# Two output gates of block 2 in seven quarter products, and the sums of weight slices by accumulating transfers

## What is computed

```
p = h @ w_in
c_val, c_gate, c_og, ts, r_og, g_conv, g_rwkv = split(p)
# convolution branch
u = layernorm(conv31(c_val * sigmoid(c_gate)))
y_c = (silu(u) * silu(c_og)) @ w_conv_out
# recurrence branch: r, k, v and the decay from ts
o = groupnorm(rwkv7(r, decay, k, v, kk, kk * a)) + bonus
y_r = (o * silu(r_og)) @ w_rwkv_out
# g_conv and g_rwkv gate y_c and y_r, and w_out follows
```

## Time and profile before

| | |
|---|---|
| median of 3 runs | 1057.2 us |
| the profiled execution's own time | 1056.02 us |
| its span, first to last instruction | 1054.2 us |
| granted TensorE clock, mean | 0.998 |
| busy in the span: TensorE, VectorE, ScalarE, GpSimd | 99%, 72%, 23%, 12% |
| a stage of block 2, pairs 2 to 6 | 46.6 us |
| TensorE's share of the chain that ended last | 97% |

### The profile page before, as it was taken

One profiled execution on the slowest core, in us unless ns is written; L12 is line 12 of the kernel. 1 busy time (PEld: TensorE's weight loads), 2 busy tenths in 40 slices (PEclk: granted clock), 3 DMA queues, 4 the chain that ended last, 5 costly groups with the idle time before them and its releaser, 6 DMA issues.

```text
span 1054.2 us, 21653 instructions
## 1 busy us (share of the span) xinstructions
PE 1043.1 (99%) x8888; PEld 902.0 (86%) x8888; DVE 757.2 (72%) x1714; ACT 237.5 (23%) x630; POOL 126.8 (12%) x174
## 2 busy tenths in 40 slices
PE   9999999999999999999999999999999999999997
PEld 8899899998988499999644988898898989887983
DVE  4488776867743477777757788777878778777875
ACT  4032222213300120010101432323232232324101
POOL 1101000000045121100250010010100001010052
PEclk9999999999999999999999999999999999999999
DMA  8786566552377447564556333233333322161261
GB/s 263 267 307 237 207 198 220 193 186 88 121 228 231 159 71 251 196 191 161 176 194 229 90 111 101 88 114 101 101 94 108 121 81 82 41 242 41 81 160 40
DMA packets 72309, 162.68 MB, mean 154 GB/s; under 512 B 18930, under 2 KB 33170, under 8 KB 72211
## 3 DMA queue, kind: packets, MB, share of 16 engines
q1 hardware_dynamic: 71202, 159.67, 46.1%
q10 hardware_dynamic: 1008, 1.63, 0.5%
HBM read 160.17 MB, written 1.11 MB: 153 GB/s over the span
## 4 chain that ended last, share of the span: by engine, by line
PE 97%; DVE 2%; DMA 1%; issue 0%; ACT 0%; POOL 0%; DVEq 0%; ACTq 0%; POOLq 0%
PE bank L861 27%; PE bank L1016 18%; PE bank L492 13%; PE bank L927 6%; PE bank L1042 4%; PE bank L678 3%; PE bank L793 2%; PE bank L836 2%; PE bank L1188 2%; PE bank L1200 2%; PE bank L1357 2%; PE bank L1079 1%; PE bank L989 1%; PE bank L995 1%; PE bank L570 1%; PE bank L523 1%
## 5 line engine op out<-in xcount | busy, mean ns | idle before, releaser
L1016 PE MATMUL bank<-hT,slots 128*128 128x256 f32 x896 | 204.9, 382 | 0.0
L1016 PEld LDWEIGHTS bank<-hT,slots 128*128 128x128 f32 x896 | 167.6, 190 | 23.3 <-issue 0.3
L861 PE MATMUL bank<-hT,slots 128*128 128x128 f32 x832 | 103.4, 275 | 0.0
L2513 DVE SCALAR_TENSOR_TENSOR arena<-padA,par,arena 128x256 f32<-128x256 f32 x232 | 102.8, 504 | 0.0
L861 PEld LDWEIGHTS bank<-hT,slots 128*128 128x128 f32 x832 | 97.9, 192 | 0.7 <-issue 0.7
L861 PE MATMUL bank<-arena,slots 128*128 128x128 f32 x768 | 95.6, 275 | 0.0
L861 PEld LDWEIGHTS bank<-arena,slots 128*128 128x128 f32 x768 | 90.9, 192 | 0.5
L492 PE MATMUL bank<-hT,slots 128*128 128x256 f32 x336 | 74.4, 380 | 0.0
L492 PEld LDWEIGHTS bank<-hT,slots 128*128 128x128 f32 x336 | 63.4, 190 | 9.2 <-issue 0.8
L492 PE MATMUL bank<-arena,slots 128*128 128x256 f32 x304 | 66.2, 379 | 0.4 <-DMA slots<-in_w_br 0.4
L492 PEld LDWEIGHTS bank<-arena,slots 128*128 128x128 f32 x304 | 57.6, 190 | 8.6 <-DMA slots<-in_w_br 0.8
(11 more groups left out here) (480 smaller groups left out, 1891.1 us busy)
## 6 DMA issues: line engine op xcount, KB each, us to landing
slots<-in_w_rwkv SPq DMA_DIRECT2D x72, 512.0 KB, 3.6
slots<-in_w_heads SPq DMA_DIRECT2D x64, 512.0 KB, 4.5
slots<-in_w_gu SPq DMA_DIRECT2D x44, 512.0 KB, 4.5
arena<-in_ada_w SPq DMA_DIRECT2D x24, 512.0 KB, 5.2
slots<-in_w_down SPq DMA_DIRECT2D x20, 512.0 KB, 4.4
slots<-in_w_br SPq DMA_DIRECT2D x32, 256.0 KB, 2.8
slots<-in_w_out SPq DMA_DIRECT2D x16, 512.0 KB, 4.1
slots<-in_w_y SPq DMA_DIRECT2D x16, 512.0 KB, 6.9
```

The source lines that it names most:

```text
L861: end = e.matmul(out, w[:, k * P:(k + 1) * P], rhs[:, k, :], start=k == 0, stop=k == 3)
L1016: end = e.matmul(proj(w, q), slot[w][:, k * P:(k + 1) * P], hT[:, k, :], start=k == 0, stop=k == KT - 1)
L2513: e.scalar_tensor_tensor(out=o, in0=src, scalar=w, in1=o, op0=ALU.mult, op1=ALU.add).then_inc(*dve.step(f"tap{n}.{q}"))
```

## The change

For pairs 0 to 6 the output gates OGP and ROG are made like the branch gates, by seven products of quarters. `own_gate_pair` becomes `own_pair(e, what, q)`, called for "o" and then for "g". The raw gates are put together in a new tile `oraw`: one copy on ScalarE, one addition on VectorE in gap 5 (`first_output_sums`), three in gap 6 (`other_output_sums`); the two tanh and the two gating operations come behind these. Signs of `bt` change, so that all sums of weight slices are plain additions, and two results come out negated (the scale of -0.5 and the subtraction take care of it).

VectorE makes no slice sum any more. SyncE loads three more quarters of 256 KB for each gate pair (`load_sums`), and GpSimd's queue issues four accumulating transfers of 256 KB for each: eight in a stage, between `Z0` and `csum`. `FILL` goes from 70 units used to 68, and a few taps are dealt out anew.

```diff
-FILL = (0, 12, 11, 12, 11, 13, 13)
-FILL_FIRST = (14, 9, 9, 10, 10, 10, 10)
+FILL = (0, 11, 11, 11, 11, 12, 12)
+FILL_FIRST = (13, 9, 9, 9, 9, 9, 10)
...
+        oraw = carve(4, P)
+        osum = [carve(512) for _ in range(2)] + [adaA[:, 2 * D + 512:]]
...
+                elif w in (OGP, ROG) and q < LAST:
+                    e.wait_ge(*dve.upto(f"oq11.{q}" if w == OGP else f"oq1221.{q}"))
...
-        def own_gate_pair(e, q):
+        def own_pair(e, what, q):
+            even, odd = PAIR_OF[what]
+            one, two = gate_banks_of(q) if what == "g" else output_banks_of(q)
+            s2, s3, s4 = bs if what == "g" else osum
...
                 if n == 2:
                     e.wait_ge(*dve.upto("bt4"))
-                    e.wait_ge(*dve.upto(f"bs4.{q}"))
+                    e.wait_ge(*added[what][1].upto(f"sum2.{q}"))
                 if n == 3:
-                    read_out(e, PLACE[GRP, q] - 2)
+                    e.wait_ge(*added[what][0].upto(f"sum1.{q}"))
+                    read_out(e, PLACE[odd, q] - 2)
+                if n == 4:
+                    e.wait_ge(*added[what][2].upto(f"sum3.{q}"))
+                if n == 5:
+                    e.wait_ge(*added[what][3].upto(f"sum4.{q}"))
...
-                for w in (OGP, ROG):
-                    yield from projection(e, w, j)
-                yield from own_gate_pair(e, j)
+                yield from own_pair(e, "o", j)
+                yield from own_pair(e, "g", j)
...
             if more:
-                slice_sum(3)
-                og_silu()
+                first_output_sums()
                 operand_b(e, j + 1)
...
             if more:
-                rg_silu()
+                other_output_sums()
                 operand_r(e, j + 1)
...
             if more:
-                taps(e, j + 1, 13 if chain else 10, 18)
+                og_silu()
+                rg_silu()
+                taps(e, j + 1, 14 if chain else 10, 17)
...
+        def slice_additions(e, what, j):
...
+            e.wait_ge(*in_slot[odd].upto(f"rw{odd}.{j}"))
+            e.dma_start(s1, from_odd[:, 512:], accum_op=ALU.add).then_inc(*added[what][0].step(f"sum1.{j}"))
+            e.wait_ge(*in_sum[what][1].upto(f"a11.{j}"))
+            e.dma_start(s3, from_odd[:, 0:512], accum_op=ALU.add).then_inc(*added[what][2].step(f"sum3.{j}"))
+        def later_additions(e, what, j):
...
+            e.dma_start(s2, s1, accum_op=ALU.add).then_inc(*added[what][1].step(f"sum2.{j}"))
+        def last_additions(e, what, j):
...
+            e.dma_start(s4, s2, accum_op=ALU.add).then_inc(*added[what][3].step(f"sum4.{j}"))
...
+            if j < LAST:
+                for additions in (slice_additions, later_additions, last_additions):
+                    for what in "og":
+                        additions(e, what, j)
...
+            def load_sums(what, j):
...
+                e.dma_start(s2, src[:, 0:512]).then_inc(*in_sum[what][0].step(f"a11.{j}"))
+                e.dma_start(s3, src[:, 0:512]).then_inc(*in_sum[what][1].step(f"a11.{j}"))
+                e.dma_start(s4, src[:, 512:]).then_inc(*in_sum[what][2].step(f"a12.{j}"))
```

More of the change, by code:

```diff
@@ L166, in build @@
         in_ada = [tally(f"loads_into_ada{n}", 16) for n in range(2)]
+        in_sum = {w: [tally(f"loads_into_sum{n}_{w}", 16) for n in range(3)] for w in "og"}
+        added = {w: [tally(f"additions_into_sum{n}_{w}", 16) for n in range(4)] for w in "og"}
         to_g = tally("stores_to_g", 16)
@@ L427, in build @@
         LAST = R_PAIRS - 1
+        PAIR_OF = {"o": (OGP, ROG), "g": (GCP, GRP)}
         NEXT, OWN = (VAL, GATE, K_, R_, V_), (OGP, ROG, GCP, GRP)
@@ L1043, in own_gate_pair @@
                     if k == 3 and n in (2, 6):
-                        end.then_inc(*pe.step(f"b126.{q}" if n == 2 else f"p{GRP}.{q}"))
+                        end.then_inc(*pe.step(f"{what}126.{q}" if n == 2 else f"p{odd}.{q}"))
                     if k % 2:
@@ L1775, in act_rwkv @@
                     act_pad(e, "v", V_, j + 1)
-                half_gate(OGP, OG[:, j, :], "og.th", j)
+                e.wait_ge(*pe.upto(f"o126.{j}"))
+                e.activation(oraw[:, 1, :], output_banks_of(j)[0][:, 0, :], ACT.Copy).then_inc(*act.step(f"op1.{j}"))
             if levels:
                 inverted(4)
-            if more:
-                half_gate(ROG, rg[j % 3], "rg.th", j)
-            if levels:
                 e.wait_ge(*pe.upto(f"tok.{j}"))
                 e.activation(tokBK[j % 2], chunks(bank[4][:, :]), ACT.Copy).then_inc(*act.step(f"tok.{j}"))
+            if more:
+                for n, (to, name) in enumerate(((OG[:, j, :], "og.th"), (rg[j % 3], "rg.th"))):
+                    e.wait_ge(*dve.upto(f"oq1221.{j}"))
+                    e.activation(to, flat(oraw[:, 2 * n:2 * n + 2, :]), ACT.Tanh, scale=0.5).then_inc(*act.step(f"{name}.{j}"))
             if last:
@@ L2663, in dve_rwkv @@
             if more:
-                slice_sum(0)
                 dve_decays(e, j + 1)
             if levels:
-                taps(e, j, *((23, 28) if not j else (27, CONV2) if more else (22, 27)))
+                taps(e, j, *((23, 28) if not j else (26, CONV2) if more else (22, 27)))
             if j and more:
@@ L3270, in sp_rwkv @@
                       OGP: BY_PRODUCT, GCP: DOWN - 2}
+            DONE_BY = {GCP: GRP, OGP: ROG}
+            def load_sums(what, j):
+                if j == 0:
+                    e.wait_ge(*pe.upto("lora"))
+                even, (s2, s3, s4) = PAIR_OF[what][0], bs if what == "g" else osum
+                src = a["w_rwkv"][j * NR + even, :, :]
+                e.dma_start(s2, src[:, 0:512]).then_inc(*in_sum[what][0].step(f"a11.{j}"))
+                e.dma_start(s3, src[:, 0:512]).then_inc(*in_sum[what][1].step(f"a11.{j}"))
+                e.dma_start(s4, src[:, 512:]).then_inc(*in_sum[what][2].step(f"a12.{j}"))
             def load_projection(w, j):
-                e.wait_ge(*pe.upto(f"p{GRP if w == GCP else w}.{j - 1}" if j else free[w]))
+                e.wait_ge(*pe.upto(f"p{DONE_BY.get(w, w)}.{j - 1}" if j else free[w]))
                 if j == 0 and w in summed:
@@ L3282, in sp_rwkv @@
                 load_projection(w, 1)
+            for what in "og":
+                load_sums(what, 0)
             for j in range(1, R_PAIRS):
@@ L3288, in sp_rwkv @@
                     load_projection(w, j)
+                    if w in (ROG, GRP) and j < LAST:
+                        load_sums("o" if w == ROG else "g", j)
         def sp_out(e):
```

89 lines of the change are left out of this document (54 added, 35 removed).

## The result

The changed kernel takes **1058.57 us** (median of 20 runs, 1057.86 to 1060.47); beside it the kernel before takes 1056.82 us (20 runs, 1055.56 to 1059.56). The ratio is 1.0018, 95% interval 1.0012 to 1.0025: 1.75 us slower where 4.5 us faster was forecast, above the upper end of the range. The profiled execution took 1058.07 us, its span is 1056.3 us.

The account below looks back on a forecast made before the run. TensorE, busy 99% of the span, was taken as the bound: 1056.0 - 4.6 + 0.1 for small waits = 1051.5 us for a profiled execution, with the median 1.2 us above it 1052.7 us, range 1051.2 to 1056.4 us.

Parts of the forecast that it names:

- The size of the gain: TensorE's rows per pair: 6.91 us of removed products become 6.26 us, 0.65 us less per pair, 4.6 us for seven.
- Nothing waits behind GpSimd's queue but `csum`: GpSimd's queue: behind the transfers only csum, read only in the last pair, and the next `Nd.m`, 40 us on.
- VectorE gains about 1.5 us against 0.43: Gaps 2 and 3: three slice sums of about 0.65 us go, one 0.41 us tap comes; gap 3 loses a unit.
- Gap 1, 0.11 us late: Gap 1 loses 0.43 us against 0.32 idle, so `state(1)` comes 0.11 us late; priced at nothing, 0.8 us at worst.
- Gap 4, nothing: Gap 4 keeps its units and gets a tap ahead of a ScalarE wait: nothing, at worst 0.4 us x 7.
- Gaps 5 and 6: VectorE's play at the ends of gaps 5 and 6: 0.29 and 0.57 us stay, so both cost nothing.
- `oq1221`: Added TensorE wait in gap 6: 0.36 us spare less a handover, taken as nothing; pair 0's wait 0.5 us.
- Transfers: Accumulating transfers taken at 4 us, between 2.8 and 9.5; the fifth in time for gap 5; DMA share about 0.6.
- Issues beside VectorE: GpSimd's eight issues beside VectorE in gaps 1 to 3: between nothing and 2.6 us a stage, taken as nothing.
- Rival 2: Gain returns as VectorE waits (gaps 1, 3, 5, `oq1221`), 0.2 to 0.6 us a pair: 1054.1 to 1057 us; chance 0.13.
- Rival 1: GpSimd's issues hold up VectorE's taps, 1.5 us a pair reaching TensorE: 1063 us; chance 0.12.
- Rivals 3 and 4: Third: transferred sums arrive late, 1081 us, chance 0.03. Fourth: rows don't get cheaper by the count, about 1057, chance 0.02.

Follow-up runs that it names:

- experiment 1: Changed kernel with csum moved ahead of the last four accumulating transfers of a stage in GpSimd's program: 1052.63 us, ratio 0.9963 to the kernel before.
- experiment 4: Changed kernel without its 56 accumulating transfers, TensorE waiting for the plain loads instead: 1053.02 us, ratio 0.9966 to the kernel before.
- experiment 3: Kernel before with csum alone held until VectorE has made kp, beside the six taps of gap 3: 1056.61 us, ratio 1.0.
- experiment 6: Kernel before with csum held until kp and one 256 KB accumulating transfer issued right ahead of it: 1059.77 us, ratio 1.0031.
- experiment 5: Changed kernel with csum behind all transfers and held until the fourth of gap 3's seven taps: 1056.85 us, ratio 1.0003 to the kernel before.
- experiment 7: Kernel before with csum held until ScalarE's square of k is done, no issue ahead: 1056.9 us, ratio 1.0004.

## Why the prediction was wrong

**The size of the gain was right.** 32 rows for 56, 0.65 us a pair: with both losses removed a middle stage is 45.96 us (45.95 was forecast). Pairs 1 to 6 together take 275.27 us there (649.21 to 924.48); the forecast is 279.19 - 6 x 0.65 = 275.29.

**Where the changed kernel's 282.20 us come from** is then a subtraction: csum early takes it to 276.57 (647.92 to 924.49), so csum's place costs 5.6 us; the longer gap 1 takes it to 275.27, so the missing play costs 1.3. Together 6.9 us against a gain of 3.9 in these six pairs. The split depends on the order: the longer gap 1 alone takes it to 279.86, which is worth 2.3, and csum's place is then worth 4.6.

**The step that failed first: "Nothing waits behind GpSimd's queue but `csum`".** It asked who needs csum's result (no one, until the last pair), and not what csum does to its neighbour when it runs 8.0 us later in the stage (at 755.08 us, 13.5 into its stage, before; at 763.69, 21.6 into it, now). Part of the price was on the table: the earlier trace rows had shown operations of GpSimd slowing taps, and I applied it to the issues alone, which by experiments 1 and 4 cost nothing by themselves. That csum costs 1.0 to 1.3 us right behind an issue, and not 0.48, no row of before could tell.

**The step that failed second: "VectorE gains about 1.5 us against 0.43"** in gaps 2 and 3. Taking work away gains time only up to the next wait. In the kernel before ScalarE's `own.k` ended at 761.07 and `shift` began at 761.10: the slice sums just filled a wait that was there anyway. Without them VectorE is idle for 1.83 us, and `shift` starts at the same 19.53 us. The whole relief was worth nothing, while TensorE's need came two units, 0.86 us, earlier and gap 3 got one more tap, 2.85 - 2.46 = 0.39 us. Play of 1.05 us became a lack of 1.05 - 0.86 - 0.39 = -0.2, and with csum early a stage is 46.15 us instead of 45.95. It is this that made csum's collision count in full; with the old play csum cost a stage nothing alone (experiment 3), and 0.24 us behind an issue (experiment 6).

**Point by point, the rest.**
- Gap 1, 0.11 us late, priced at nothing: no wait there. Gap 4, nothing: right.
- Gaps 5 and 6: 0.30 and 0.53 us of idle time against 0.29 and 0.57.
- `oq1221`: no wait in pairs 1 to 6; pair 0's stall 0.5 us, as worked out.
- Transfers: I took 4 us between 2.8 and 9.5; they took 4.3 to 8.1. In time for TensorE, as said. But the size mattered in a way that I had not asked: it sets when csum runs. In pair 6, with quicker ones, csum falls into VectorE's idle time and costs nothing.
- Issues beside VectorE: nothing, as taken. The second half of the rule of the Trainium skill ("SBUF — State Buffer", Who interferes with whom), which no row of before showed, fits here, if an issue is a thing that only writes: seven taps beside one take 2.85 us, as without. By its first half csum's new neighbours had to be looked at too, and I did not.
- Rival 2, the gain coming back as waits on VectorE, is what happened, at 1 us a pair instead of 0.2 to 0.6, and in gap 3, where I had counted a surplus. Rival 1 had GpSimd holding up VectorE right, and the wrong instruction of GpSimd. Rivals 3 and 4 did not occur. The measured slowdown, 0.17%, is just within the 0.2% that I had called no change, to which I gave 0.08.

## What to carry to other kernels

When work is put into a queue ahead of something harmless, ask not only who waits for the harmless one but what it will then run beside, and move it out of the way in the program's order. When work is taken off an engine, read what that engine waits for next before the time is booked as a gain: here ScalarE's pass ended 0.07 us after the removed work. And read the play of the place where engines meet, before and after: 1.05 us of it would have taken up nearly all of a collision that cost 1 us a pair once it was gone.

## What the runs showed of the hardware

- A `tensor_tensor` of GpSimd over 256 columns (0.73 to 0.85 us) beside VectorE's two-input operations makes one of them, the next to start, end 0.3 us after it: 0.95 to 0.97 us instead of 0.47, a loss of 0.47 to 0.49 us, in three runs (experiments 3, 5 and 7) and at two phases.
- With a transfer's issue right ahead of it (records 0.3 us into each other) it holds the first operation of VectorE that starts 0.10 us or more after the issue's start: 1.40 to 1.80 us instead of 0.43 or 0.47, a loss of 1.0 to 1.3 us, in both kernels, 16 times of 16. I had not expected an issue, itself free, to double the cost of what follows it.
- The same operation beside a `reciprocal` costs nothing (1.75 us), beside a `tensor_scalar` with one tensor as input 0.28 us (0.70 instead of 0.41).
- An accumulating transfer of 256 KB that reads HBM lands 7.8 to 8.1 us after its issue in the changed kernel, where four are issued in a row; the single one of experiment 6, also from HBM, lands after 4.3 (medians). From SBUF to SBUF it is 4.3 to 6.1. The issue takes GpSimd 0.86 us, and 1.15 to 1.89 with another right ahead. The 512 KB loads beside them went from 3.6 to 4.5 us, with no effect on TensorE.
